# Attention of the later layers: probabilities divided before they are turned, the sink as one more key, no turning back

## The reference, cut to what matters

```python
def sliding_window_attention(q, k, v, sinks):      # B=1, S=512, H=8, KV=2, D=64, W=128
    ...
    s = jnp.einsum('bnqkgd,bnskd->bnkgqs', qb, kb_kk) * (D ** -0.5)
    s = jnp.where(valid, s, -jnp.inf)
    mx = jnp.maximum(jnp.max(s, axis=-1, keepdims=True), sink)
    p = jnp.exp(s - mx)
    denom = jnp.sum(p, axis=-1, keepdims=True) + jnp.exp(sink - mx)
    o = jnp.einsum('bnkgqs,bnskd->bnqkgd', p / denom, vv)

def token_mixer(h, ...):
    ...
    a_out = sliding_window_attention(q, k, v, attn_sinks)
    y = jnp.concatenate([m_out, a_out], axis=-1)    # m_out: a recurrent mixer with 4 heads of 128
    return y @ w_out
```

## Time and profile before

| what | value |
|---|---|
| median of 3 runs | 2767.23 us (2767.2 to 2769.93) |
| the profiled execution | 2768.16 us |
| its span, first to last instruction | 2766.3 us |
| PE busy | 2609.0 us, 94% |
| DVE, ACT, POOL busy | 1219.6, 880.6, 852.4 us |
| the 12 jobs with the attention, first later layer | 1656.24 to 1753.45 |
| the same, second later layer | 2229.30 to 2326.50 |

### The profile page before, as it was taken

One profiled execution on the slowest core, in us unless ns is written; L12 is line 12 of the kernel. 1 busy time (PEld: TensorE's weight loads), 2 busy tenths in 40 slices (PEclk: granted clock), 3 DMA queues, 4 the chain that ended last, 5 costly groups with the idle time before them and its releaser, 6 DMA issues.

```text
span 2766.3 us, 36753 instructions
## 1 busy us (share of the span) xinstructions
PE 2609.0 (94%) x14332; PEld 1850.0 (67%) x14332; DVE 1219.6 (44%) x2420; ACT 880.6 (32%) x1671; POOL 852.4 (31%) x1166
## 2 busy tenths in 40 slices
PE   9999999999988888888888899999999999999999
PEld 7888777888533333334333367788888887888887
DVE  6433745225633333333333357553441565644422
ACT  4433335322211111111111144553332446433332
POOL 5343434552000000000000043345555435345554
PEclk9999999999999999999999999999999999999999
DMA  4223222336999999999999951122332221123322
GB/s 159 79 100 105 72 76 77 104 122 257 414 427 427 428 429 428 429 429 429 428 428 428 426 178 66 50 92 92 94 115 95 90 100 61 62 91 106 108 92 76
DMA packets 128151, 571.99 MB, mean 207 GB/s; under 512 B 11152, under 2 KB 58640, under 8 KB 102928
## 3 DMA queue, kind: packets, MB, share of 16 engines
q1 hardware_dynamic: 122768, 560.82, 51.0%
q10 hardware_dynamic: 5248, 9.32, 1.1%
HBM read 565.86 MB, written 4.26 MB: 206 GB/s over the span
## 4 chain that ended last, share of the span: by engine, by line
PE 68%; DMA 23%; DVE 5%; ACT 2%; issue 1%; POOL 0%; SPq 0%; ACTq 0%; DVEq 0%
PE ps L392 43%; DMA wide<-in_moe_w 16%; PE ps L1577 8%; DMA arena<-in_moe_w 7%; PE ps L2105 3%; PE ps L2084 2%; PE ps L2074 1%; PE ps L2125 1%; PE ps L673 1%; PE ps L708 1%; PE ps L689 1%; PE ps L2091 1%; PE ps L1353 1%; PE ps L937 0%; POOL ring_r L349 0%
## 5 line engine op out<-in xcount | busy, mean ns | idle before, releaser
L349 POOL TENSOR_TENSOR ring_r<-ring,ring_r 128x256 fp32r<-128x256 f32 (+2 forms) x1136 | 833.7, 773 | 1818.3 <-ACT ring_r L332 1818.3
L392 PE MATMUL ps<-xnT_r,ring_r 128*128 128x512 f32 (+1 forms) x1664 | 483.9, 374 | 0.0
L392 PE MATMUL ps<-ring_r,xnT_r 128*128 128x512 f32 (+1 forms) x1296 | 412.7, 389 | 3.0 <-DVE xn_r L3171 2.5
L392 PEld LDWEIGHTS ps<-xnT_r,ring_r 128*128 128x128 f32 x1664 | 304.4, 188 | 56.6 <-issue 1.3
L392 PE MATMUL ps<-ring_r,arena_r 128*128 128x512 f32 x1392 | 323.9, 391 | 0.0
L392 PE MATMUL ps<-xn_r,ring_r 128*128 128x512 f32 (+1 forms) x832 | 310.2, 373 | 0.0
L332 ACT ACTIVATE ring_r<-ring 128x1024 fp32r<-128x1024 f32 (+2 forms) x284 | 272.4, 1025 | 88.7 <-DMA ring<-in_w_down 67.4
L392 PEld LDWEIGHTS ps<-ring_r,arena_r 128*128 128x128 f32 x1392 | 259.9, 188 | 56.4 <-issue 2.2
L392 PEld LDWEIGHTS ps<-ring_r,xnT_r 128*128 128x128 f32 x1296 | 251.0, 200 | 49.9 <-issue 5.7
L2105 PE MATMUL ps<-wide,arena 128*32 128x512 f32 x752 | 192.0, 657 | 90.5 <-DMA wide<-in_moe_w 90.5
L2105 PEld LDWEIGHTS ps<-wide,arena 128*32 128x32 f32 x752 | 51.8, 118 | 229.5 <-issue 210.8
(11 more groups left out here) (407 smaller groups left out, 3491.2 us busy)
## 6 DMA issues: line engine op xcount, KB each, us to landing
wide<-in_moe_w SPq DMA_DIRECT2D x143, 2048.0 KB, 32.9
arena<-in_moe_w SPq DMA_DIRECT2D x46, 2048.0 KB, 32.9
ring<-in_w_in SPq DMA_DIRECT2D x22, 2048.0 KB, 8.3
ring<-in_w_up SPq DMA_DIRECT2D x20, 2048.0 KB, 8.6
ring<-in_w_down SPq DMA_DIRECT2D x10, 2048.0 KB, 7.8
ring<-in_w_in SPq DMA_DIRECT2D x16, 512.0 KB, 4.9
ring<-in_w_out SPq DMA_DIRECT2D x4, 2048.0 KB, 8.5
ring<-in_w_ret_branch SPq DMA_DIRECT2D x2, 2048.0 KB, 9.0
```

The source lines that it names most:

```text
L349: ins = nc.gpsimd.tensor_tensor(ring_r[:, q % 2, piece], ring[:, q % 2, piece], ring_r[:, 2 + q % 2, piece].bitcast(F32), ALU.subtract)
L392: ins = nc.tensor.matmul(bank, left, right, start=(start and k == 0), stop=(stop and k == 2))
```

## The change

The sink becomes one more column of a half's scores: DVE copies it beside the masked scores, the maximum runs over 257 columns and comes out negated, and the exponential's sum holds the sink. DVE takes the reciprocal of the sums (`window_share_dve`), ACT multiplies the probabilities by it in token rows (`window_scale_act`), and only then PE turns them. Scores and probabilities have four buffers in place of two. Since the values then come out divided, nothing is turned back: ACT and DVE store the high and low parts straight from bank 6 (`window_high_act`, `window_low_dve`), and the rows of `w_out` are loaded in the order of the heads, as two transfers of 64 partitions. "back", "a_turn" and `window_end_dve` go. The turn moves four chunks later in the list (`off == 4`), the scaling stands at `off == 5` and the tile's end at `off == 2`.

```diff
                         if off == 0 and 0 <= p <= W + 1:
                             if p >= 2:
                                 yield "values", p - 2
-                            if 1 <= p <= W:
-                                yield "turn", p - 1
-                            if 2 <= p <= W and tile_of_pair(window, p - 2) is not None:
-                                yield "back", tile_of_pair(window, p - 2)
                             if p < W:
                                 yield "scores", p
-                        if off == 2 and p == W + 1:
-                            yield "back", NT - 1
-                        if n == len(J.order) - 1 and c in (2, 5):
-                            yield "a_turn", 2 * (c // 3)
-                            yield "a_turn", 2 * (c // 3) + 1
+                        if off == 4 and 1 <= p <= W:
+                            yield "turn", p - 1
+                        if off == 5 and 0 <= p < W:
+                            yield "scale", p
+                        if off == 2 and 2 <= p <= W + 1 and tile_of_pair(window, p - 2) is not None:
+                            yield "tile_done", tile_of_pair(window, p - 2)
...
+            elif kind == "heads":
+                dst = ring[:, layer_slot(q)].rearrange("p (c n) -> p c n", n=D)
+                sp.dma_start(dst[FIRST_HALF], src[0]).then_inc(att_rows_loaded, 16)
+                dst, src = dst[SECOND_HALF], src[1]
...
+        def window_mask_dve(v, n):
+            i, heads, wide, m0 = window_chunk(n)
+            v.wait_ge(Z.scores_ready, n + 1)
+            if n >= 4:
+                v.wait_ge(Z.probs_ready, n - 3)
+            s = Y.masked[:, n % 4]
+            nc.vector.tensor_copy(s[:, :, wide], Y.sinks[:, heads])
+            nc.vector.tensor_tensor(s[:, :, 0:wide], ps[:, window.score_bank[n % 2], 0:2 * wide].rearrange("p (h k) -> p h k", h=2),
+                                    window.mask[:, None, m0:m0 + wide].to_broadcast([P, 2, wide]), ALU.add).then_inc(Z.scores_taken, 1)
+            v.wait_ge(Z.scores_taken, n + 1)
+            nc.vector.tensor_reduce(top_of(n), s[:, :, 0:wide + 1], AX.X, ALU.max, negate=True).then_inc(Z.max_ready, 1)
...
+        def window_share_dve(v, n):
+            i, heads, _, _ = window_chunk(n)
+            v.wait_ge(Z.probs_ready, n + 1)
+            total = window.totals[:, i, heads]
+            nc.vector.reciprocal(total, total).then_inc(shares_ready, 1)
+
+        def window_scale_act(a, n):
+            i, heads, wide, _ = window_chunk(n)
+            a.wait_ge(shares_ready, n + 1)
+            for j in range(2):
+                at = j * (SPAN + 1)
+                probs = Y.probs[:, n % 4, at:at + wide]
+                ins = nc.scalar.activation(probs, probs, ACT.Copy, scale=window.totals[:, i, heads.start + j:heads.start + j + 1])
+            ins.then_inc(probs_scaled, 1)
...
+        def window_high_act(a, i):
+            mixed, cols = tile_columns(i)
+            a.wait_ge(Z.mixed_ready, (i + 1) * window.per_tile)
+            nc.scalar.activation(Y.aT[0][cols], mixed, ACT.Copy).then_inc(Z.out_kept, 1)
+
+        def window_low_dve(v, i):
+            mixed, cols = tile_columns(i)
+            v.wait_ge(Z.out_kept, i + 1)
+            nc.vector.tensor_tensor(Y.aT[1][cols], mixed, Y.aT[0][cols].bitcast(F32), ALU.subtract).then_inc(Z.mixed_taken, 1)
```

More of the change, by code:

```diff
@@ L773, in attend_mixed_act @@
             bank = ps[:, A.mixed_bank[i % len(A.mixed_bank)], :]
[L774 to L778, removed]
+            nc.scalar.activation(A.res[:, i, 0:BANK], bank, ACT.Copy).then_inc(Z.mixed_taken, 1)
         def tile_of_pair(A, p):
@@ L2848, in project_pe @@
                     attend_pair_values_pe(pe, window, k)
[L2849 to L2857, removed]
         def rope_tile_dve(v, n):
@@ L2932, in project_dve @@
                     for n in (2 * k, 2 * k + 1):
-                        attend_mask_dve(v, link, window, n)
-                    if n == len(window.chunks) - 1:
-                        window_sinks_dve(v)
+                        window_mask_dve(v, n)
+                elif what == "scale":
+                    for n in (2 * k, 2 * k + 1):
+                        window_share_dve(v, n)
                 elif what == "turn":
@@ L2938, in project_dve @@
                         attend_keep_dve(v, window, n)
[L2939 to L2942, removed]
-                    nc.vector.tensor_tensor(Y.aT[1][:, :, k * P:(k + 1) * P], ps[:, 2 + k % 2, :].rearrange("p (c k) -> p c k", c=4),
-                                            Y.aT[0][:, :, k * P:(k + 1) * P].bitcast(F32), ALU.subtract).then_inc(Z.out_low, 1)
+                elif what == "tile_done":
+                    window_low_dve(v, k)
         def project_act(a):
@@ L2992, in project_act @@
                     for n in (2 * k, 2 * k + 1):
-                        attend_exp_act(a, window, n)
-                    if n == len(window.chunks) - 1:
-                        window_end_act(a)
+                        window_exp_act(a, n)
+                elif what == "scale":
+                    for n in (2 * k, 2 * k + 1):
+                        window_scale_act(a, n)
                 elif what == "values" and tile_of_pair(window, k) is not None:
-                    attend_out_T_act(a, window, tile_of_pair(window, k))
-                elif what == "back":
-                    attend_mixed_act(a, window, k)
-                elif what == "a_turn":
-                    a.wait_ge(Z.out_turned, k + 1)
-                    nc.scalar.activation(Y.aT[0][:, :, k * P:(k + 1) * P], ps[:, 2 + k % 2, :].rearrange("p (c k) -> p c k", c=4), ACT.Copy).then_inc(Z.out_kept, 1)
+                    window_high_act(a, tile_of_pair(window, k))
         def gate_logs_act(a):
@@ new lines, in window_chunk, with top_of @@
+        def window_chunk(n):
+            i, heads, keys, m0 = window.chunks[n]
+            return i, heads, keys[-1][0].stop - keys[0][0].start, m0
+        def top_of(n):
+            at = 16 + 2 * (n % 4)
+            return small[:, at:at + 2]
+        def window_mask_dve(v, n):
[9 more added lines that the diff above has]
+            nc.vector.tensor_reduce(top_of(n), s[:, :, 0:wide + 1], AX.X, ALU.max, negate=True).then_inc(Z.max_ready, 1)
```

72 lines of the change are left out of this document (35 added, 37 removed).

## The result

The changed kernel takes **2778.62 us** (median of 5 runs, 2776.84 to 2780.52), 1.0039 times the time of before (95% interval 1.0027 to 1.005; with two more runs the median of before is 2767.2). The forecast was 2780. The profiled execution took 2777.5 us; the page gives its span and PE's busy time.

What follows compares the result with a forecast made beforehand. PE, busy 94% of the span, was taken as the bound. Waits of 9.8 less 5.1 removed give 4.7 a layer, 9.4 in both; clock falls add 3.4: 2767.2 + 12.8 = 2780 us, range 2768 to 2789.

Steps and rivals of the forecast that it cites:

- What goes, 5.1 a layer: On PE, the turnings back, the waits ahead of them and the a_turns go: 5.1 us less per layer.
- ACT's scalings fit: ACT's 32 multiplications a layer, at most 16 us, fit beside PE in sum and order; nothing counted.
- The split load is hidden: Loading `w_out` as two transfers, even at 15.6 us, delays nothing, as ACT's rounding comes later still; nothing counted.
- The new waits: PE's values wait for DVE's late keep: 1.0, 2.6, 2.5 and 3.7, 9.8 us a layer, bounds 7.9 and 12.3.
- One fall of the clock per layer, behind the longest wait: Behind round 5's wait of 3.7 us PE runs a stretch at 1.2 GHz: 1.7 us a layer, 3.4 in both.
- Rival 1: No fall of PE's clock, only the net waits: 2776.6 us; chance 0.25.
- Rival 2: Each of a layer's three longer PE waits (rounds 2, 3, 5) brings a clock fall: 19.6 us more, 2787; chance 0.15.
- Rival 3: DVE's chains are shorter, so PE's waits of 5 a layer eat the 5.1 removed: 2767, no change; chance 0.12.
- rival 4: DVE's keeps are in time and only PE's removed transposes count: 2757 us, faster; chance 0.10.

Runs made afterwards that it cites:

- values_late: The changed kernel with the values of a pair four chunks later and the tile's end at off 6: 2758.89 us, 0.9967 of the kernel before.
- no_scaling: The changed kernel without ACT's 32 multiplications a layer, turns waiting for the exponentials alone, reciprocals kept: 2777.8 us.
- scans_late: The changed kernel with DVE's five operations behind the `lf` row moved behind the keep of pair 4 and the reciprocals that follow: 2768.52 us.
- turn_early: The changed kernel with the turn put back to off 0, behind the values and ahead of the scores, scaling still at off 5: 2797.14 us.
- two_buffers: The changed kernel with two buffers for scores and probabilities in place of four, with the waits to match: 2790.94 us.
- streaming_all: The changed kernel with 7, 9 and 15 matmuls on the unit matrix, computing nothing, ahead of the values of pairs 1, 2 and 4: 2773.62 us.
- again: The changed kernel itself measured once more, on the same chip as the run with all waits filled: 2778.13 us.
- streaming: The changed kernel with 24 calls of matmuls on the unit matrix, computing nothing, ahead of the values of pair 4 only: 2776.33 us.
- both_late: The changed kernel with the values four chunks later and DVE's scans behind the keep: 2760.18 us.

## Why the prediction was right

- **What goes, 5.1 a layer: right.** `values_late` has the work of the changed kernel and no wait: 92.73 - 87.45 = 5.3. The 1.3 for the waits was the wait of the weight loads. PE's own idle time there was only 0.49 and 0.31, but by starts the larger number is the right one: the two turnings back began 1.69 and 1.74 us behind the turns ahead of them (1682.27 and 1720.06), which take 1.02 where nothing waits, so 1.4 was lost.

```profile
1683.96 0.66 PE L718 MATMUL ps<-cst,arena 128*128 128x128 f32 x4 [0.49 <-ACT arena L769]
...
1721.80 0.66 PE L718 MATMUL ps<-cst,arena 128*128 128x128 f32 x4 [0.31 <-ACT arena L769]
```

- **ACT's scalings fit: right.** A multiplication of 256 columns took 1.71 / 4 = 0.43 (bound 0.49); no turn waits for ACT in the changed kernel, and `no_scaling` changes nothing.

```profile
1695.00 1.71 ACT L3372 ACTIVATE arena<-arena,small 128x256 f32<-128x256 f32 x4 [4.25 <-DVE small L3364]
```

- **The split load is hidden: right.** It was issued at 1731.44 and 1732.12 and took a median of 9.9 us to land. ACT rounded the unit from 1746.92.

```profile
1731.44 0.64 SPq L2643 DMA_DIRECT2D ring<-in_w_out  x1
1732.12 0.62 SPq L2654 DMA_DIRECT2D ring<-in_w_out  x1
```

- **The new waits: right in place, releaser and number, somewhat too large.** 0.41, 1.93, 2.34 and 3.86, together 8.5, against 1.0, 2.6, 2.5 and 3.7, together 9.8. In round 1 the masks were not 0.6 late but began as the scores ended (1667.99 and 1667.95). In round 2 the two small copies took 0.45 and 0.16, not 0.5 each, so the masks ended earlier. In round 5 the `lf` work took 6.2, not 5.75.
- **One fall of the clock per layer, behind the longest wait: right in number, place and size (1.5 for 1.7), but not in its ground.** The prediction let the length decide: 3.7 is longer than 2.75, the other waits are shorter. The experiments show falls behind 1.88 (`scans_late`) and 1.41 (`turn_early`) and none behind 3.07 (`two_buffers`), so it is partly luck that this term came out. Rival 1 falls with it. Rival 2 (a fall behind each longer wait) is wrong for the changed kernel; `turn_early` came near it, with a fall behind four of its five waits of more than 1.3 us.
- **The sum.** 92.73 - 5.3 + 8.5 + 1.5 = 97.4 against the measured 97.06, so 4.3 a layer in place of the forecast 6.4: 1.3 of the difference are the smaller waits, 0.2 the larger removal, 0.2 the smaller fall, and 0.4 is that waits of 8.5 us of idle time made the stretch only 95.51 - 87.45 = 8.1 longer (`streaming_all`, whose values start as late as in the changed kernel and which has no fall, against `values_late`). The profiled span grew by 9.4, of which 8.7 are these two stretches. The medians differ by 11.4, since the profiled execution of before was 1.0 above its median and that of the changed kernel 1.1 below. No term of the prediction stands for that, so the forecast, 2 us a layer too high in its terms, is within 1.4 us of the median partly by luck.
- **Rivals 3 and 4** needed waits of about 5 a layer or fewer. (Rival 3's 2767 also lay just outside the range, which the prediction doesn't say.) `values_late` shows what rival 4 described, 2757 predicted and 2758.9 measured, once PE asks later.

What the runs show as the cause: PE asks for the keep before DVE, in the written order, has come to it. A later question takes all four waits away (`values_late`), and a shorter list ahead takes away the longest (`scans_late`). For the other three, whose keeps stand behind masks and taps, a shorter list was not tried.

## What to carry to other kernels

When a step moves later in a list that all engines walk, look at the consumer of its result too: here the turn moved by four chunks and the values did not, so the copy between them lost half its time and landed behind everything else on DVE. Moving the consumer by two chunks turned a loss of 0.4% into a gain of 0.3%. For each engine in the chain write down what stands ahead of the moved step in its own order and set that length against the time until the next engine asks; that gave the places of all four waits before anything ran. Here the work removed from the bounding engine counted in full (5.3 us a layer for the 5.1 forecast), but only once no new wait stood in its place.

## What was not expected of the hardware

The length of PE's wait alone does not decide whether the clock falls. Waits of 3.86 were followed by a fall in both layers of the changed kernel, of `again` and of `no_scaling`. Waits of 1.87 to 1.93 were not in these, but were in `scans_late` (1.88, both layers) and in `streaming` (1.87, second layer). In the first layer of `streaming` the fall behind 2.34 came before the filled place, after the same work and waits as in the changed kernel, where there was none; so these don't decide it either. A fall behind 1.41 was seen too (`turn_early`), none behind 1.29 (`both_late`), and none behind 3.07 (`two_buffers`, first layer).

The clock also fell where the profile shows no wait of PE at all. In the first layer of `both_late` PE is busy for all of 1715 to 1752 at a granted clock of 1.00. Then, at the start of the next stage, the clock falls, and fifteen products take 5.30 us, where `values_late` has 3.70 (the window gives length, PE busy, clock, DMA share and GB/s):

```profile
1752.00:1756.00 4.00, 4.00 (x12) 0.59 0.39 111
1752.61 5.30 PE L395 MATMUL ps<-ring_r,extra_r 128*128 128x512 f32 x15
```

```profile
1751.37 3.70 PE L395 MATMUL ps<-ring_r,extra_r 128*128 128x512 f32 x15
```

The second layer of `no_scaling` and the first of `two_buffers` show the same 5.30. These falls lie behind the end of the length that the table compares.

The Trainium skill (TensorE: Matmul & The Clock Gate, "HAM oscillation — how this bites in real kernels") says that gaps which are too long start the next burst throttled, each time anew: `turn_early`, with four falls, agrees for the most part, the changed kernel, with one fall behind three long waits, less so, and the fall in `both_late` follows no gap that the profile shows. What picks the place stays open. A fall cost 1.5 us where it could be measured by itself (`again` against `streaming_all`).
